# An mLSTM/GLA/attention step: log decays inside two heads, three projections at GLA's head, value rows by DMA

## What is computed

```python
def gla_chunked(q, k, v, log_a, s0):
    ...
    def step(s, chunk):
        qc, kc, vc, lac = chunk
        bc = jnp.cumsum(lac, axis=2)
        o_inter = jnp.einsum('bhtk,bhkv->bhtv', qc * jnp.exp(bc), s)
        decay = jnp.exp(jnp.where(mask, bc[:, :, :, None, :] - bc[:, :, None, :, :], -jnp.inf))
        a = jnp.einsum('bhtk,bhsk,bhtsk->bhts', qc, kc, decay)
        o = o_inter + jnp.einsum('bhts,bhsv->bhtv', a, vc)
        b_end = bc[:, :, -1]
        s_new = jnp.exp(b_end)[..., None] * s + jnp.einsum('bhsk,bhsv->bhkv', kc * jnp.exp(b_end[:, :, None, :] - bc), vc)
        return s_new, o
...
def rec_mixer(h, w_in, b_mgate, w_gate_up, b_gate, m_norm_g, g_norm_g, w_out, c0, n0, m0, s0):
    ...
    hm, c, n, m = mlstm_chunkwise(heads(mq, M_HEADS), heads(mk, M_HEADS) * M_HEAD_DIM ** -0.5,
                                  heads(mv, M_HEADS), mi, mf, c0, n0, m0)
    hm = rms_norm(hm, m_norm_g) * jax.nn.sigmoid(heads(mo, M_HEADS).astype(f32))
    log_a = jax.nn.log_sigmoid((glr @ w_gate_up + b_gate).astype(f32)) / G_GATE_TAU
    hg, s = gla_chunked(heads(gq, G_HEADS) * G_KEY_DIM ** -0.5, heads(gk, G_HEADS), heads(gv, G_HEADS),
                        heads(log_a, G_HEADS), s0)
    hg = rms_norm(hg, g_norm_g) * jax.nn.silu(heads(gg, G_HEADS).astype(f32))
```

## Time and profile before

| | |
|---|---|
| three runs | 1560.1, 1562.2, 1564.9 us (median 1562.2) |
| profiled execution | 1559.6 us, its span 1557.8 us |
| TensorE busy | 1429.0 us, 92% of the span |
| VectorE, ScalarE, POOL busy | 55%, 34%, 7% |
| head 1, first matmuls | 105.2 us |
| head 2, head 3 | 153.6 us, 206.3 us |
| gate matmuls after head 3 | 250.5 us |
| g_kd transposes, pair 0 and pair 1 | 275.9 us, 310.3 us |
| output projection starts | 343.7 us |

### The profile page before, as it was taken

The page is one execution under the profiler, slowest core; times in us unless marked ns, Lnnn a source line. Parts: engine busy times, 40 slices in busy tenths (PEclk is TensorE's granted clock), DMA queues, the critical chain, the costliest instruction groups (busy, mean ns, idle before and its releaser), DMA issues.

```text
span 1557.8 us, 29793 instructions
## 1 busy us (share of the span) xinstructions
PE 1429.0 (92%) x11857; PEld 1345.6 (86%) x11857; DVE 864.0 (55%) x1332; ACT 531.4 (34%) x857; POOL 109.2 (7%) x133
## 2 busy tenths in 40 slices
PE   5999996789999999999999888897699999999997
PEld 4898895569899999999998667675599999999997
DVE  5455448623566666632253888878545666665221
ACT  4333423323422332322234554544243323232110
POOL 0111101201100000000101000010020000000000
PEclk9999998669999999999999999998699999999999
DMA  5444232102222222332225445565022222223320
GB/s 194 83 137 124 58 121 84 44 17 68 82 91 89 91 94 94 106 98 91 72 86 203 166 166 168 181 208 176 5 96 82 95 94 87 91 96 114 113 88 21
DMA packets 44188, 162.57 MB, mean 104 GB/s; under 512 B 5546, under 2 KB 6874, under 8 KB 43866
## 3 DMA queue, kind: packets, MB, share of 16 engines
q1 hardware_dynamic: 38506, 143.77, 28.5%
q0 software_dynamic: 5616, 17.86, 3.5%
HBM read 150.18 MB, written 11.43 MB: 104 GB/s over the span
## 4 chain that ended last, share of the span: by engine, by line
PE 80%; DVE 10%; ACT 4%; issue 4%; DMA 0%; POOL 0%; DVEq 0%; ACTq 0%; POOLq 0%
PE ps L507 56%; PE ps L558 12%; DVE mx L1842 2%; DVE s_sc L1874 1%; PE ps L944 1%; ACT e_att L1289 1%; ACT w_hi L1013 1%; PE ps L868 1%; PE ps L920 1%; PE ps L607 1%; DVE e_att L1855 1%; DVE ps L1839 1%; DVE a_att L1859 1%; PE ps L677 1%; PE ps L789 1%
## 5 line engine op out<-in xcount | busy, mean ns | idle before, releaser
L507 PE MATMUL ps<-h_hi,w_hi 128*128 128x260 f32 x1744 | 496.8, 285 | 9.6 <-DVE h_lo L1398 4.6
L507 PE MATMUL ps<-h_hi,w_lo 128*128 128x260 f32 x1744 | 494.9, 284 | 0.0
L507 PE MATMUL ps<-h_lo,w_hi 128*128 128x260 f32 x1744 | 493.4, 283 | 0.0
L1389 DVE TENSOR_TENSOR w_lo<-raw,w_hi 128x1024 fp32r<-128x1024 f32 (+1 forms) x189 | 244.0, 1291 | 416.6 <-ACT w_hi L1013 416.3
L507 PEld LDWEIGHTS ps<-h_hi,w_hi 128*128 128x128 f32 x1744 | 330.6, 190 | 11.9 <-issue 9.4
L507 PEld LDWEIGHTS ps<-h_lo,w_hi 128*128 128x128 f32 x1744 | 330.4, 189 | 0.2
L507 PEld LDWEIGHTS ps<-h_hi,w_lo 128*128 128x128 f32 x1744 | 330.4, 189 | 0.0
L1013 ACT CAST w_hi<-raw 128x1024 fp32r<-128x1024 f32 (+1 forms) x189 | 208.1, 1101 | 238.8 <-PE ps L507 232.7
L507 PE MATMUL ps<-a_lo,w_hi 128*128 128x260 f32 x704 | 199.0, 283 | 0.0
L507 PE MATMUL ps<-a_hi,w_hi 128*128 128x260 f32 x704 | 198.7, 282 | 0.0
L507 PE MATMUL ps<-a_hi,w_lo 128*128 128x260 f32 x704 | 198.7, 282 | 0.0
(11 more groups left out here) (361 smaller groups left out, 2007.2 us busy)
## 6 DMA issues: line engine op xcount, KB each, us to landing
raw<-in_w_ffn SPq DMA_DIRECT2D x88, 512.0 KB, 3.5
raw<-in_w_down SPq DMA_DIRECT2D x32, 704.0 KB, 4.1
k_pages<-in_cache_k SPq DMA_DIRECT2D x32, 512.0 KB, 3.5
v_pages<-in_cache_v SPq DMA_DIRECT2D x32, 512.0 KB, 6.0
raw<-in_w_rec_in SPq DMA_DIRECT2D x29, 512.0 KB, 5.7
raw<-in_w_att_kv SPq DMA_DIRECT2D x24, 512.0 KB, 3.5
raw<-in_w_rec_out SPq DMA_DIRECT2D x8, 512.0 KB, 3.4
raw<-in_w_att_q SPq DMA_DIRECT2D x8, 512.0 KB, 3.4
```

The lines of the kernel that those rows point to most:

```text
L507: ins = TE.matmul(half(bank, h), w_part[:, buf, w], m_part[:, k_at + k, h * HALF:(h + 1) * HALF], start=start, stop=stop)
L1389: V.tensor_tensor(w_lo[:, n % 2, 0:nk * P], raw[:, n % RAW, 0:nk * P], w_hi[:, n % 2, 0:nk * P].bitcast(F32), ALU.subtract).then_inc(lo_sp ...
```

## The change

`HEAD_SLABS` gets six, five, five and five slabs; tiles 17, 19 and 22 come last (`GLA_SLABS`). The gate matmuls of pair p run in head 1 + p (`DECAY_HEADS`), behind `part(3)`. Tiles 17 and 19 of `z` hold the log decays until their own slabs are drained, tile 22 is scratch. "lf" is done in the head after. The Silu moves from head 2 to head 3. The scaling of the queries in tile 16 moves into head 3, that of tile 17 behind `factors(0)`; the split of slab 28 goes behind the first scan, and those of the first two output slabs around `h_lo`. The samples' value rows go to memory element by element (`v_rows`) and come back broadcast into `g_vb`; `g_dv` and its matmuls are gone.

```diff
-HEAD_SLABS = [[13, 1, 5, 9, 24, 25], [14, 2, 6, 10, 26, 27], [15, 3, 7, 11, 16, 17], [18, 19, 20, 21, 22, 23]]
+HEAD_SLABS = [[13, 1, 5, 9, 24, 25], [14, 2, 6, 10, 26], [15, 3, 7, 11, 27], [16, 18, 20, 21, 23]]
+GLA_SLABS = [17, 19, 22]
```

TensorE in a head, and then in the GLA part:

```diff
+                if h - 1 in DECAY_HEADS:
+                    wait(pe, lD, "z", DECAY_HEADS.index(h - 1))
...
                 part(3)
+                if h in DECAY_HEADS:
+                    p = DECAY_HEADS.index(h)
+                    wait(pe, mD, "cn3", h)
+                    for n in range(2):
+                        ins = TE.matmul(half(0, n), c_("w_gate_up")[64:80, p * P:(p + 1) * P],
+                                        gates[64:80, n * HALF:(n + 1) * HALF], start=True, stop=True)
+                    ins.then_inc(lP.sem, 1)
...
-                if h < M_HEADS - 1:
+                if len(HEAD_SLABS[h]) > 5:
                     part(5)
```

```diff
-            part(PER_HEAD - 1)
-            pe.wait_ge(drained, S_REC_IN)
-            wait(pe, lD, "z")
+            pe.wait_ge(drained, GLA_FIRST)
+            slab_part(GLA_FIRST, GLA_FIRST % 2, range(KT), 2)
+            wait(pe, mA, "rms", M_HEADS - 1)
+            slab_part(GLA_FIRST + 1, (GLA_FIRST + 1) % 2, range(KT), 4)
...
+                if p == 0:
+                    pe.wait_ge(drained, GLA_FIRST + 1)
+                    slab_part(GLA_FIRST + 2, (GLA_FIRST + 2) % 2, range(KT), 2)
                 wait(pe, dD, "kd", p)
...
-                for n in range(2):
-                    for hh, half_ones in ((0, c_("ones_lo")), (1, c_("ones_hi"))):
-                        ins = TE.matmul(ps[:, n, :], half_ones,
-                                        g_dv[:, hh, 4 * n:4 * n + 4, :].rearrange("p b v -> p (b v)"),
-                                        start=hh == 0, stop=hh == 1)
```

ScalarE, at a head's end and in the GLA part:

```diff
+                if h in DECAY_HEADS:
+                    p = DECAY_HEADS.index(h)
+                    wait(act, lD, "neg", p)
+                    S.activation(z[:, 22, :], z[:, 22, :], ACT.Exp).then_inc(lA.sem, 1)
+                    wait(act, lA, "exp", p)
+                    S.activation(z[:, 22, :], z[:, 22, :], ACT.Ln, bias=one[:, :]).then_inc(lA.sem, 1)
                 rec_step(first + 4)
...
+                    if p == 0 and name == "far":
+                        rec_step(GLA_FIRST + 1)
...
-            rec_step(S_REC_IN - 1)
+            wait(act, qD, "la")
+            rec_step(GLA_FIRST)
             decays(0)
```

VectorE, near the start and the end of a head:

```diff
                 rec_split(1)
+                if h - 1 in DECAY_HEADS:
+                    p = DECAY_HEADS.index(h - 1)
+                    wait(dve, lA, "ln", p)
+                    V.scalar_tensor_tensor(out=z[:, 17 + 2 * p, :], in0=z[:, 17 + 2 * p, :], scalar=0.0, in1=z[:, 22, :],
+                                           op0=ALU.min, op1=ALU.subtract).then_inc(lD.sem, 1)
...
+                if h in DECAY_HEADS:
+                    p = DECAY_HEADS.index(h)
+                    log_p = z[:, 17 + 2 * p, :]
+                    wait(dve, lP, "up", p)
+                    V.tensor_scalar(two(log_p), pair(0), p_("b_gate", p, 1), None, ALU.add).then_inc(lD.sem, 1)
+                    wait(dve, lD, "z", p)
+                    V.scalar_tensor_tensor(out=z[:, 22, :], in0=log_p, scalar=-1.0, in1=log_p, op0=ALU.mult,
+                                           op1=ALU.min).then_inc(lD.sem, 1)
```

POOL, called for tiles 20, 21 and 23 and then, behind the load of `g_ss`, for tile 22:

```diff
+            def value_rows(tile):
+
+                pool.wait_ge(drained, REC_TILES.index(tile) + 1)
+                pool.dma_start(a["v_rows"][tile - 20].rearrange("b k -> k b"), z[:, tile, T:NT],
+                               allow_slow_non_contiguous=True).then_inc(v_rows_out, 16)
```

104 lines of the change are left out of this document (53 added, 51 removed).

## The result

The changed kernel took 1567.2 us (median of 20 executions, 1559.5 to 1573.9), the kernel before 1562.5 (20 executions beside it, 1559.2 to 1568.8). The ratio is 1.0027, with a 95% interval of 1.0014 to 1.0039: **slower by 0.27%**, just inside the 0.3% that counts as no change, where 13.4 us less were forecast. The profiled execution of the changed kernel is its slowest: 1573.9 us with a span of 1571.5, against a span of 1557.8 before. So 13.7 us between the two profiles stand for 4.7 between the medians.

A forecast was written before the change was run, and what follows sets the result against it. TensorE, busy 92% of the span, was taken as the bound, leaving its idle time, low clock and own work. GLA head 6.9, heads 5.3 and value rows 1.2 sum to 13.4 us: 1548.8 us, range 1542 to 1557.

The forecast's parts named there:

- GLA's head, +6.9: From head 3's last sum to the g_kd transposes: log decays moved into heads 1 and 2 shorten it by 6.9 us.
- neg: VectorE step in heads 1 and 2: 0.6 to 0.7 us for half the width, not 2.2, without POOL arithmetic beside it.
- The pause at the heads' starts: After heads 1 and 2 lose their last slab, TensorE idles 3.4 us waiting for ScalarE's root before the next head.
- the next head starts at 151.7 instead of 153.65: End of head 1: the next head starts earlier, winning 1.9 us of the 5.8 removed.
- Rival (a): Idleness before small matmuls at both changed head starts costs more clock, the tail gains none: gain 7.8 us, 1554.4; chance 0.19.
- Silu and "lf": Silu leaves head 2 for head 3, "lf" costs 0.6 us in each: head 2 gains 4.3 us, head 3 loses 0.9.
- the price is nothing: Element DMAs on POOL's queue, 7 us each: row 22 lands about 276.5, leaving 5 us to spare, so no cost.
- The value rows, +1.2: L735 matmuls leaving TensorE: pair 0 loses 1.0 us, pair 1 wins 3.2 less 1.0 for clock, so 1.2 us gained.
- (b): Value rows come late if each DMA costs above 8.5 us; samples 4.2 us late at 10.4: 1553.0 us; chance 0.12.
- (c): Slower than before through POOL's queue, each microsecond per DMA counting four at the end: 1567 us; chance 0.05.
- (d): Slabs at GLA's head don't hide and TensorE idles between them; with 5 us late, 1553.8 us; chance 0.06.
- the prediction's three signs of being wrong: POOL's memset ends after the far levels, g_kv waits for its rows, or neg takes over 1 us.

The follow-up runs named there:

- e2: The changed kernel with the value rows taken back to TensorE (g_dv and the L735 matmuls): 0.9988 of the kernel before, 1560.8 us.
- e6: The changed kernel with seven dummy matmuls at the ends of heads 1 and 2: 0.9983 of the kernel before, 1559.5 us.
- e13: e10 without its dummy matmuls: 0.9944 of the kernel before, 1556.3 us.
- e10: The changed kernel, rows by DMA, with row 22 behind pair 0's far levels, exp and ln behind the root, and e7's dummy matmuls: 0.9889, 1547.2 us.
- e1: The kernel before with only the value rows changed to element DMAs and broadcasts, without L735 matmuls: 0.9984 of the kernel before, 1561.1 us.
- e5: The changed kernel with value rows on TensorE again and exp and ln behind the root (e2 and e4 together): 0.9972, 1557.1 us.
- e11: As e8, but row 22's 4 KB go out as 128 pieces of 32 bytes instead of 1024 of 4: 0.9971, 1561.0 us.
- e7: e5 with four dummy matmuls each at the ends of heads 1 and 2 and five ahead of pair 0's wait for g_ss: 0.9923, 1550.0 us.
- e14: e10 with row 22 sent early again, ahead of pair 0's near levels: 0.9906 of the kernel before, 1551.3 us.
- e15: e10 with pair 0's two broadcasts into g_vb also issued behind its far levels: 0.9876 of the kernel before, 1545.5 us.
- e4: The changed kernel with exp and ln of heads 1 and 2 behind the root on ScalarE: 1.0001 of the kernel before, 1561.9 us.
- e8: e2 plus an element DMA of row 22 that nobody needs, issued where the changed kernel issues it: 1.0040 of the kernel before, 1569.8 us.

## Why the prediction was wrong

**GLA's head, +6.9: right.** 6.8 measured. The "neg" of 520 columns took 0.70 us; the rule of the Trainium skill (page SBUF — State Buffer, section "SBUF: two separate sides") that was weighed there held, and e2 shows it again with the scan, 5.05 us beside GpSimd's spreads and 1.23 without.

**The pause at the heads' starts: right in size, wrong in price.** 3.24 us against the 3.4 forecast, in place of 5.7 to 5.9 of slab. But heads 1 to 3 together came out 2.9 us longer instead of 5.3 shorter. The step that failed is "the next head starts at 151.7 instead of 153.65": it counts the pause and not what TensorE does behind it. The first matmuls went from 2.9 to 5.0 and from 3.2 to 5.6, and the slab behind them ran at 0.50. Rival (a) named this, with one stretch of 1.7 us for each head. The granted clock was low for 6.8 us more at each head, which costs half of that, 3.4; e6 and e13 give 3.3 us for each. In the medians the fillers took 0.44% off the changed kernel (e6) and 0.55% off the repaired one (e13, e10). The forecast had given (a) a chance of 0.19 against its own row, which said that a stretch came right after 2.1 us of idleness. That row should have set the sum. In head 1, which has no such pause at its start, only 0.5 us of the 1.9 came. There the changed kernel's profile has a low stretch from 113.9 to 117.3 that neither before nor e2 has, and e2, with the same code in head 1, was 2.0 us shorter: the 1.9 was right.

**Silu and "lf".** No idleness is left behind the Silu in head 2, and c_n is waited for 1.5 us at most, both as forecast. With the fillers alone (e6) heads 1 and 2 were 0.5 and 4.2 us shorter than before and head 3 0.8 longer, against 1.9, 4.3 and 0.9 forecast. With the root first as well (e10) they were 3.2, 5.4 and 0.7 us shorter, 9.2 together: more than the 5.3 forecast, 2.4 of it from the shorter pause, which the forecast did not have. The mechanism was right where the clock held.

**The element DMA, "the price is nothing": the second step that failed, and the largest error.** The time of one, 7 us, was 10.4, at the upper bound. Its landing was only compared with those that wait for it by semaphore: the memset, the broadcast. There the cover held, with the memset done at 289.5 and the far levels at 297.9. The cost came at TensorE, which waits for nothing of it: 9.37 us. The forecast had read the sign of it, "near levels wait 7.5 us for nothing that the profile shows", and used it only to bound what the clock could give. It should have asked what those waits were for. They come at an even distance: of the 384 near matmuls that a profile records for pair 0, 178 stand before one wait and 306 before the next in the kernel before, the changed one, e1, e2, e5, e11 and e13, and 162 and 290 in e7, e10, e14 and e15. That is 128 apart each time. And the page has a DMA queue for instructions (queue: packets, MB, share of 16 engines), in the changed kernel as

```profile
q8 instruction: 48, 0.79, 0.2%
```

which is some 16 KB a packet. The DMA view of a narrow stretch tells when such a packet moved. The long wait of the changed kernel is from 282.35 to 291.72. From 281 to 289 us the view has

```profile
DMA packets 104, 0.42 MB, mean 53 GB/s; under 512 B 1, under 2 KB 1, under 8 KB 104
q1 hardware_dynamic: 104, 0.42, 44.9%
```

and from 289 to 290

```profile
DMA packets 100, 0.36 MB, mean 361 GB/s; under 512 B 15, under 2 KB 15, under 8 KB 99
q1 hardware_dynamic: 99, 0.34, 99.2%
q8 instruction: 1, 0.02, 5.9%
```

So from 281 us until the element DMA had landed (issued at 277.0, landed by 287.4) the other queues crept, and no instruction packet moved; the last had gone at 278.4. Then one did, over by 290.1, and TensorE went on 1.6 us later. It is the same elsewhere. The 17 traces of this case have 65 waits of TensorE of over 1 us without a releaser between 250 and 335 us; 63 of them end 1.2 to 1.8 us after such a packet's end, the short ones of the kernel before too (1.4 and 1.5). For the other two, one in e4 and the 3.8 us in e8, no packet is recorded near. So the waits are for instructions, as far as times can show it, and the element DMA made the packet late. That the small pieces do this was shown by e8 and e11; where in the DMA engines the packet is held, no view shows.

On this DMA the Trainium skill, page DMA: Bandwidth & Descriptors, section "Specifications", was cited for its rule on transfers below 512 bytes. The runs agree on the direction and add a step within it: 4 KB in pieces of 4 bytes took about 10.4 us, in pieces of 32 bytes 2.4, both far below 512.

**The value rows, +1.2: not borne out, and the sign stays open.** L735's 4.69 us left pair 1's chain, and only 0.5 us of it came back in the outputs, since L757 then waited 1.75 us for g_s and ran at low clock, 3.75: 2.2 was forecast. Pair 0's samples took 1.6 us more, with 1.0 forecast. With samples and rec_out the tail of pair 1 was 25.7 us in the changed kernel and 21.3 before. But this is one profile, and the tail moves by as much from profile to profile: 21.6 to 25.8 in the eight kernels with the change and rows by DMA, 21.5 to 25.3 in the six with the change and rows on TensorE. So it can't be put down to the rows. In the repaired kernel the rows by DMA came out ahead, 0.9876 against 0.9923, with intervals that touch, so that is not settled either. How much of it is L735 itself stays open, as the spreads on GpSimd go with it.

**The rivals.** (b) and (c) had the right culprit, one slow element DMA, and sought its victim in GpSimd's queue. (d) did not occur: the three slabs filled TensorE. The result on the slower side came by a mechanism that no rival held, and none of the prediction's three signs of being wrong came: the memset was in time, g_kv did not wait for its rows, and "neg" took 0.70. With both failed steps repaired (e15) the kernel was 17.7 us under the one before, where 13.4 had been forecast, with dummies and an order of ScalarE and GpSimd that the forecast did not have.

## What to carry to other kernels

When idle time replaces work of the same length, count what runs behind it at the lower clock, and where the idleness cannot be removed, put work of no use into it: 13 dummy matmuls gave 9 us here. Place a DMA of many small pieces by who else uses the DMA engines at that time and not only by who waits for its data, and keep it away from stretches of many tiny matmuls. A wait of TensorE with no releaser that recurs at an even distance is a resource to be named before anything is put beside it.
